# Moving a second layer's conditioning chunks from the first projections into two norms and a later stage, with three expert chunks loaded ahead, in a two-layer fp32 trunk

## What is computed

```
c_act = silu(c)
for l in range(2):
    mod = c_act @ w_ada[l] + b_ada[l]                 # 24 chunks of 1 MB a layer: "conditioning"
    sh1, sc1, gt1, sh2, sc2, gt2 = split(mod, 6)
    h = x * (1 + sc1) + sh1
    y = token_mixer(h, ...)                           # one input projection w_in, gMLP and HGRN2 heads, w_out
    x = layer_norm(ALPHA * x + gt1 * y)
    h = x * (1 + sc2) + sh2
    f = swiglu(h) if l == 0 else moe_swiglu(h)        # dense of width 2816, then top-2 of 8 experts
    x = layer_norm(ALPHA * x + gt2 * f)
```

## Time and profile before

| what | value |
|---|---|
| runs before | 1508.42, 1511.43, 1513.97 us |
| the profiled execution | 1511.0 us, of which the span from the first to the last instruction is 1509.2 us |
| mean granted TensorE clock | 0.984 |
| PE busy | 1458.1 us, 97% of the span |
| DVE busy | 1168.5 us, 77% |
| ACT busy | 908.6 us, 60% |
| POOL busy | 46.3 us, 3% |
| share of the chain that ended last | PE 56%, DVE 3%, issue 1%, ACT 1% |
| HBM | 275 GB/s over the span |

### The profile page before, as it was taken

How to read it: one execution, slowest core, us unless ns; L and a number is a source line. 1 busy time by engine, 2 the same in 40 slices (tenths; PEclk the granted TensorE clock), 3 DMA queues, 4 the chain that set the end, 5 groups by cost and what they waited for, 6 DMA issues and landing times.

```text
span 1509.2 us, 24798 instructions
## 1 busy us (share of the span) xinstructions
PE 1458.1 (97%) x9804; PEld 1271.8 (84%) x9804; DVE 1168.5 (77%) x1244; ACT 908.6 (60%) x867; POOL 46.3 (3%) x84
## 2 busy tenths in 40 slices
PE   5999999999999999999999999999999999999995
PEld 4899988999998998867888888888878888888884
DVE  1556786556668667859889889898898898988988
ACT  1646565323334665656777676776766766777774
POOL 2000110000000100010000000000000000000000
PEclk7999999999999999999999999999999999999998
DMA  9999467455445742547999999999999999999995
GB/s 329 355 310 338 136 205 262 127 167 167 140 139 188 239 133 64 171 141 255 353 350 352 334 362 337 342 356 333 353 342 333 363 336 341 355 344 365 349 369 194
DMA packets 217751, 416.21 MB, mean 276 GB/s; under 512 B 7919, under 2 KB 79769, under 8 KB 217638
## 3 DMA queue, kind: packets, MB, share of 16 engines
q1 hardware_dynamic: 214086, 402.31, 76.6%
q0 software_dynamic: 3552, 12.33, 2.7%
HBM read 407.80 MB, written 6.82 MB: 275 GB/s over the span
## 4 chain that ended last, share of the span: by engine, by line
PE 56%; DVE 3%; issue 1%; ACT 1%; DMA 0%; DVEq 0%; ACTq 0%
PE bank L702 16%; PE bank L704 16%; PE bank L703 16%; PE bank L1233 1%; PE bank L1271 1%; PE bank L705 1%; PE bank L707 1%; PE bank L706 1%; DVE w_lo L1819 1%; PE bank L1326 1%; PE bank L1327 1%; PE bank L849 0%; PE bank L1182 0%; DMA raw_ring<-in_e_gate_dram 0%; PE bank L1066 0%
## 5 line engine op out<-in xcount | busy, mean ns | idle before, releaser
L1819 DVE TENSOR_TENSOR w_lo<-raw_ring,w_hi 128x2048 fp32r<-128x2048 f32 x265 | 606.6, 2291 | 96.2 <-ACT w_hi L1511 95.6
L1511 ACT ACTIVATE w_hi<-raw_ring 128x2048 fp32r<-128x2048 f32 x266 | 510.5, 1919 | 230.0 <-PE bank L704 219.4
L702 PE MATMUL bank<-w_hi,xg_hi 128*128 128x512 f32 (+1 forms) x768 | 293.2, 382 | 1.2 <-DVE w_lo L1819 1.0
L704 PE MATMUL bank<-w_hi,xg_lo 128*128 128x512 f32 (+1 forms) x768 | 288.9, 376 | 0.0
L703 PE MATMUL bank<-w_lo,xg_hi 128*128 128x512 f32 (+1 forms) x768 | 288.8, 376 | 0.0
L705 PE MATMUL bank<-act_hi,w_hi 128*128 128x320 f32 x720 | 227.2, 316 | 6.2 <-DVE act_lo L1874 5.7
L706 PE MATMUL bank<-act_lo,w_hi 128*128 128x320 f32 x720 | 223.2, 310 | 0.0
L707 PE MATMUL bank<-act_hi,w_lo 128*128 128x320 f32 x720 | 223.1, 310 | 0.0
L1810 DVE TENSOR_TENSOR w_lo<-raw_ring,w_hi 128x2048 fp32r<-128x2048 f32 x65 | 148.6, 2288 | 69.0 <-ACT w_hi L1425 68.9
L704 PEld LDWEIGHTS bank<-w_hi,xg_lo 128*128 128x128 f32 x768 | 144.3, 188 | 29.2
L702 PEld LDWEIGHTS bank<-w_hi,xg_hi 128*128 128x128 f32 x768 | 144.4, 188 | 27.1 <-DVE w_lo L1819 1.4
(11 more groups left out here) (369 smaller groups left out, 1856.2 us busy)
## 6 DMA issues: line engine op xcount, KB each, us to landing
raw_ring<-in_e_gate_dram SPq DMA_DIRECT2D x90, 1024.0 KB, 5.2
raw_ring<-in_e_up_dram SPq DMA_DIRECT2D x90, 1024.0 KB, 5.3
raw_ring<-in_e_down_dram SPq DMA_DIRECT2D x88, 1024.0 KB, 5.3
raw_ring<-in_w_ada_dram SPq DMA_DIRECT2D x32, 1024.0 KB, 7.4
raw_ring<-in_w_in_dram SPq DMA_DIRECT2D x24, 1024.0 KB, 7.2
raw_ring<-in_w_ff_gate_dram SPq DMA_DIRECT2D x11, 1024.0 KB, 5.4
raw_ring<-in_w_ff_up_dram SPq DMA_DIRECT2D x11, 1024.0 KB, 5.2
raw_ring<-in_w_ff_down_dram SPq DMA_DIRECT2D x11, 1024.0 KB, 4.9
```

The source lines that it names most:

```text
L702: pe.matmul(out, xh, wh, start=start, stop=False)
L704: return pe.matmul(out, xl, wh, start=False, stop=stop)
L1511: act.activation(w_hi[:, (NSPLIT + i) % SPL, :], raw[:, s, :], ACT.Copy).then_inc(hi_ready.sem, 1)
L1819: dve.tensor_tensor(w_lo[:, r, :], raw[:, s, :], w_hi[:, r, :].bitcast(F32), ALU.subtract).then_inc(lo_ready.sem, 1)
```

## The change

1. **First projections of layer 0.** `GROUPS` no longer holds four of its pairs: one of two at w = 6, and those at w = 8, 9 and 10. Layer 0's own chunks to 23 stay. `modulation(0, 1)` follows at w = 8.
2. **Norms.** `LATE` is (8, 8, 4, 4): chunks 24 to 31 in norm (0, 0), 32 to 39 in norm (0, 1) and `win_first`, 40 behind w = 3 of layer 1 and 41 to 43 behind w = 9, m = 1; 44 to 47 stay in norm (1, 0). All `keep_busy` calls go. Layer 1's chunks are taken in another order (`ada_chunk`), so that what `modulation(1, 1)` needs is complete with 43.
3. **Slots.** The moved chunks are loaded into seven buffers that are dead at that time (`spare`), each with its own wait in SP's list (`spare_free`).
4. **DVE.** `modulation(1, 0)` goes from layer 0's output projection to chunk c = 1 of the dense channel mixer; `modulation(1, 1)` from w = 1 of layer 1's projections to the head of layer 1's output projection.
5. **ACT.** The two copies `ada_rows` behind `modulated` of layer 1 move inside it.
6. **Experts.** Chunks 4, 5 and 6 are loaded before the loop into three buffers (`ahead_sil`, `ahead_y`, `behind_hf`). The first buffer is that of `sil`, so the first silu waits until chunk 4 has been split. At the end of a round SP waits for the last scatter and loads the three again, and the fifth output waits for these loads.
7. Semaphores of the final norm are merged.

```diff
-    for w in range(2, NWIN - 1):
-        if w == 6:
-            tok = WIN_ORDER[w] // 2 in (1, 4)
-            GROUPS.update({(w, 0): 2, (w, NT - 1 if tok else 1): 2})
-        else:
-            GROUPS.update({(w, 1): 2})
-    LATE = (6, 6, RAW)
+    GROUPS.update({(w, 1): 2 for w in range(2, 8)})
+    LATE = (8, 8, 4, RAW)
...
+    LATE_GROUPS = {(3, 1): [LATE_AT[2]], (9, 1): [LATE_AT[2] + j for j in (1, 2, 3)]}
...
+    def ada_chunk(i):
+
+        l, c = divmod(i, NADA)
+        if l == 0:
+            return l, c
+        return l, c + {3: 4, 4: 3}.get(c // 4, c // 4) * 4 - c // 4 * 4
...
+            if s == EXTRA:
+                return [(qs_mm.sem, qs_mm.at(l, H - 1))]
+            if s == EXTRA + 1:
+                return [(osum_ready.sem, osum_ready.at(l, 1))]
+            if s == EXTRA + 2:
+                return [(mix_lo.sem, mix_lo.at(l, NT))]
+            if s == EXTRA + 3:
+                return [(ix_ready.sem, ix_ready.at(l, H - 1)), (oT_mm.sem, oT_mm.at(l, NT - 1)), (cv_out.sem, 32 * (l + 1))]
+            return [(h_lo.sem, h_lo.at(0, 7))]
...
             def experts(rd):
-                for i in range(RAW, NR + RAW):
-                    expert_load(i % NR, rd * NR + (NSPLIT + i - RAW + 1))
+                for i in list(range(RAW + EARLY, NR)) + list(range(RAW)):
+                    sp.wait_ge(lo_ready.sem, rd * NR + (NSPLIT + moe_before[i] + 1))
+                    expert_load(i)
+                sp.wait_ge(sc_mm.sem, sc_mm.at(rd, NE * KD - 1))
+                for i in range(RAW, RAW + EARLY):
+                    expert_load(i)
...
                         if l and kk in (1, 3):
-                            ada(LATE_AT[1] + (4 if kk == 1 else 5), turn=False)
-                        if l and kk in (3, 7):
+                            ada(LATE_AT[1] + (6 if kk == 1 else 7), turn=False)
+                        if l and kk in (1, 5):
                             ada_turn()
...
                     ada_group(l, w, m)
-                    if (l, w, m) == (0, NWIN - 1, 0):
+                    if l and w == 10:
+                        ada_turn()
+                    if (l, w, m) == (0, MOD_AT, 0):
                         ada_turn()
...
             def norm_end(l, i):
 
-                n0 = LATE_AT[2 * l + i]
+                n0 = LATE_AT[3 * l + i]
                 for j in range(2):
                     ada(n0 + j, turn=False)
                 for m in range(4 if i else KD - 2, KD, 2):
                     pair_sums(l, i, m)
-                if i:
-                    statistics(l, i)
-                    ada_turn()
-                    keep_busy(bank[5], 8)
-                    spread_root(l, i)
-                    keep_busy(bank[5], 8)
-                    ada(n0 + 2, turn=False)
-                    keep_busy(bank[5], 16)
-                    ada(n0 + 3, turn=False)
-                    return
                 ada(n0 + 2, turn=False)
                 statistics(l, i)
                 ada_turn()
                 ada(n0 + 3, turn=False)
                 spread_root(l, i)
                 if l == 0:
-                    keep_busy(bank[7], 12)
+                    for j in range(4, 6):
+                        ada(n0 + j, turn=False)
                 pe.wait_ge(stat_act.sem, stat_act.at(l, 5 * i + ROOT_COPIED))
-                if LATE[2 * l + i] > 4:
-                    ada(n0 + 4, turn=False)
                 ada_turn()
-                if LATE[2 * l + i] > 5:
-                    ada(n0 + 5, turn=False)
+                if l == 0 and i == 0:
+                    for j in range(6, 8):
+                        ada(n0 + j, turn=False)
+                    ada_turn()
...
+                    if l == 0 and i and a < 2:
+                        ada_rows(LATE_AT[0] + 5 + 2 * a)
+                    if l and i == 0 and a in (0, 2):
+                        ada_rows(LATE_AT[1] + 5 + a)
...
                 if l:
-                    ada_rows(LATE_AT[1] + 3)
-                    ada_rows(LATE_AT[1] + 5)
                     make_hi(base + 2)
...
+                if n == 0:
+                    act.wait_ge(lo_ready.sem, rd * NR + (NSPLIT + RAW + 1))
                 act.activation(sil2[:, b % 2, 0:w], bank[1 + b % 2][:, 0:w], ACT.Silu).then_inc(e_silu.sem, 1)
...
-                    if w == 1 and l:
-                        modulation(l, 1)
+
...
                 make_lo(base + 1)
+                if l:
+                    modulation(l, 1)
...
-                    if m == 1 and l == 0:
-                        modulation(1, 0)
...
+                        if c == 1:
+                            modulation(1, 0)
                         product(c)
```

More of the change, by code:

```diff
@@ L147, in hybrid_trunk @@
         landed[key] = (s, 16 * times[s])
-    RAW_USES = times[:RAW]
-    MOE_RAW0 = ring
-    assert NR % SPL == 0 and NR % RAW == 0 and all(w % CW == 0 for _, w in EB)
+    EARLY = 3
+    AHEAD0 = NSLOTS
+    times += [0] * EARLY
+    moe_slots, moe_turns, moe_before, uses, last_in = [], [], [], [0] * len(times), [None] * len(times)
+    for i in range(NR):
+        s = AHEAD0 + i - RAW if RAW <= i < RAW + EARLY else (ring + i - (0 if i < RAW else EARLY)) % RAW
+        moe_slots.append(s)
+        moe_turns.append(uses[s])
+        moe_before.append(last_in[s])
+        uses[s] += 1
+        last_in[s] = i
+    for i in range(RAW):
+        moe_before[i] = last_in[moe_slots[i]]
+    assert NR % SPL == 0 and all(w % CW == 0 for _, w in EB)
     with ExitStack() as ctx:
@@ L243, in hybrid_trunk @@
             sil, aa = (a[:].rearrange("p c n -> p (c n)")[:, 0:2 * T] for a in (sil2, aa2))
+            with ExitStack() as cx:
+                ff_spare = sb("ff_spare", [P, 3, SLOT], c=cx)
+            spare += [ff_spare[:, i, :] for i in range(3)]
             lg = sb("lg", [P, 8, NT, NE], c=c2)
@@ L286, in hybrid_trunk @@
         lt_exp = signal("lt_exp")
-        raw_in = [signal(f"raw_in{i}") for i in range(RAW + 2)]
+        raw_in = [signal(f"raw_in{i}") for i in range(AHEAD0 + EARLY)]
         hi_ready = signal("hi_ready")
@@ L412, in hybrid_trunk @@
         f_by_rs = signal("f_by_rs")
-        out_done = [signal(f"out_done{i}") for i in range(2 * NT)]
+        rows_done = signal("rows_done")
+        pool_rows_done = signal("pool_rows_done")
         outs = signal("outs")
@@ L472, in load @@
                     sp.wait_ge(lo_ready.sem, old[1] + 1)
-                what = ("ada",) + divmod(key[1], NADA) if key[0] == "ada" else split_keys[key[1]]
+                if s >= EXTRA:
+                    for free in spare_free(s, 0):
+                        sp.wait_ge(*free)
+                what = ("ada",) + ada_chunk(key[1]) if key[0] == "ada" else split_keys[key[1]]
                 sp.dma_start(slot_as(raw_slot(s), what[0]), chunk_source(*what)).then_inc(raw_in[s].sem, 16)
@@ L515, in _ @@
                 if n < RAW:
-                    sp.wait_ge(raw_in[n].sem, rounds * (16 * NR // RAW) + 16 * (RAW_USES[n] + 1))
-                sp.wait_ge(out_done[n].sem, 1)
+                    sp.wait_ge(*expert_in(rounds, n))
+                elif n == RAW:
+                    for i in range(RAW, RAW + EARLY):
+                        sp.wait_ge(*expert_in(rounds, i))
+                if n in POOL_OUT:
+                    sp.wait_ge(pool_rows_done.sem, POOL_OUT.index(n) + 1)
+                else:
+                    sp.wait_ge(rows_done.sem, n - len(POOL_OUT) + 1)
                 dst = y_prompt[0, t0:t0 + nt, cols] if t < 2 else y_sample.rearrange("b s d -> (b s) d")[:, cols]
@@ L741, in ada_group @@
             def ada_group(l, w, m):
-                for i in group_ada.get((w, m), []) if l == 0 else []:
-                    ada(i)
+                for i in (LATE_GROUPS if l else group_ada).get((w, m), []):
+                    ada(i, turn=(l == 0))
             def split_chunk(key):
@@ L1562, in _ @@
                             ada_rows(i)
+                        if (l, w, m) == (1, 10, 0):
+                            ada_rows(LATE_AT[2] + 3)
                     if w == 1:
```

129 lines of the change are left out of this document (76 added, 53 removed).

## The result

The changed kernel has a median of 1516.35 us over 12 runs (1513.93 to 1518.26), the kernel before 1511.47 us over 12 (1508.42 to 1516.03). The ratio is 1.0028, with a 95% interval of 1.0017 to 1.0039: it is slower, by 4.2 us by the ratio and 4.9 by the medians, and outside the predicted range of 1501.5 to 1513.5. (The ratio is worked out from all executions and isn't that of the two medians; the two can differ by some 2 us.) Its profiled execution took 1514.17 us with a span of 1512.4, 3.2 more than that of before.

What follows compares the result with a forecast made beforehand. PE was taken as the bound, busy 97% and without a gap in the experts. Terms −4.4 − 1.1 − 0.1 + 0.65 + 0.85 + 1.0 = −3.1 gave 1508.4 us on the median's footing, range 1501.5 to 1513.5.

Steps and rivals of the forecast that it cites:

- first projections: Layer 0's first projections: four pairs leaving them change the time by −4.4 us, bounds −8.8 and −2.2.
- norm (0, 0): Norm (0, 0): PE's DMA wait goes and the modulation leaves DVE, together −1.1 us.
- norm (0, 1): Norm (0, 1): `act_lo` ends it, not the dummies; −0.1 us without a clock fall, bounds −0.3 and +1.1.
- head and projections of layer 1: Layer 1's head: new 2.1 us stall for `w_lo` and added chunks, partly given back; +0.65 us, bounds −1.0 and +2.7.
- output projection: Layer 1's output projection: the modulation on DVE delays PE's first sums, +0.85 us, bounds 0 and 1.45.
- first silu: Start of the experts: the first silu waits for chunk 4's split, +1.0 us, bounds 0 and 1.8.
- end of the loop: End of a round: three added 1 MB loads cost 0, or +3 us if they land after the fifth output leaves.
- The first rival: First projections: all of the pairs' time, 8.8 us, comes back, giving 1502.9 us; chance 0.2.
- The −2.25: Layer 0, w = 8 to 11: without three pairs it behaves as layer 1, −2.25 us with the clock's fall.
- −3.9: The same stretch of layer 0 without the clock's fall: −3.9 us (2.25 + 1.7).
- The second rival: Clock falls ahead of layer 1's first product and in the stall before L792: 1511.8 up to 1515.2 us; chance 0.22.
- Early chunks: Start of the experts' loop: chunks loaded ahead bring at most the 0.8 us that PE waits there.

Runs made afterwards that it cites:

- run 1: Changed kernel with the slots put right: expert chunk i from 7 on in ring slot i mod 4; 1509.80 us, ratio 0.9981 to the kernel before.
- run 3: Changed kernel without its part in the experts: no chunk loaded ahead, no added wait at the first silu; 1509.13 us, ratio 0.9972.
- run 4: As run 1, with ACT's second copy at the head of layer 1 behind all four parts of the modulation; 1506.62 us, ratio 0.9957.
- run 5: As run 1, with 14 dummy products on PE in the stall for `w_lo`; 1508.46 us, ratio 0.9981; again 1508.07 us, ratio 0.9977.
- run 9: As run 8, with expert chunks 4 and 5 loaded ahead, slots put right, no wait at the first silu; 1502.02 us, ratio 0.9940.
- run 2: Kernel before, with chunk 0's reload waiting for the split of the round's last expert chunk; 1518.27 us, ratio 1.0031.
- run 8: Changed kernel without its experts part, copy behind four parts, modulation (1, 1) in w = 10, layer 0's last pair at w = 9; 1502.43 us, ratio 0.9940.
- run 1 repeated: The kernel of run 1 measured once more, on one chip with the repeat of run 5; 1508.77 us, ratio 0.9986.

## Why the prediction was wrong

The sum was right to the end of the loop and had one term there at nothing that was 6.3 us.

| term | predicted | by the rows |
|---|---|---|
| first projections | −4.4 | −4.8 (of which 0.2 was there ahead of it) |
| norm (0, 0) | −1.1 | −1.0 |
| norm (0, 1) | −0.1 | +0.4 |
| head and projections of layer 1 | +0.65 | +0.4 |
| output projection | +0.85 | +0.75 |
| first silu | +1.0 | +1.2 |
| sum up to the last round's end | −3.1 | −3.1 |
| end of the loop | 0 | +6.3 |

That −3.1 met −3.1 is in part luck. The terms are off by up to 0.5 us and cancel, and the clock of the profiled execution did what the sum had assumed: low behind the wait for `S` in layer 0, high at the two new idle stretches. In the profiles of runs 1, 3, 4, 5 and 9 it fell in other places, at 1.3 to 1.6 us each.

- **The step that failed** is the end of a round: "At the end of a round three 1 MB loads are added after the last scatter ... 0, or +3 if they don't." I looked at the loads that were added and not at those whose slot was moved. The term was put at 0, and it measured +6.3. Taking three chunks out of a ring of four shifts each later chunk by three, and the first reload of the next round then hangs on the round's last chunk. The price is one DMA's landing (6.09 us of ACT's wait), because ACT's copies of the next round stand ahead of this round's last `y_hi`. Runs 1 and 2 show it.
- **First projections: right.** PE idles 2.44 us for `S` at 145.56, as layer 1's row said, and three pairs bring 2.2 us and not 6.6. The first rival, all of the pairs' time, is ruled out; run 8 shows the other side of it, a pair that costs 0.5 us there. (The rival's own sum had the first silu at 0 where mine had +1.0, without a reason; with it, it is 1503.9.) The −2.25 was that of a low clock, and the clock was low here (0.50 from 146 to 148 us); in the profiles where it wasn't, PE left the place some 1.6 us sooner, near the −3.9 that the prediction gave for that case.
- **Norm (0, 0): right.** The DMA wait is gone, and the first product waits 0.15 us for `act_lo`.
- **Norm (0, 1): off by 0.5.** PE waited 1.63 us for a DMA into `ff_spare` ahead of the last chunk, and that chunk with its turn ran until the first product at 480.69, while `act_lo` was ready at 480.12. So the chunk's load, which I had taken as early enough, ended the norm, some 0.4 us late (an estimate from these rows). I had also misread: the first product at 486.10 shows no wait, it follows the last chunk (485.08 and 1.08 long), and `act_lo` was ready at 485.71. The clock stayed at 1.00 behind it, as I had chosen over the rule of the Trainium skill; but in the profiles of run 4, of run 5 and of run 9 it was 0.50 there, at a cost of 1.3 to 1.5 us. The choice held for this execution and not for the kernel.
- **Head of layer 1: right** (+0.4 for +0.65). ACT stood 4.60 us at the copy, `w_lo` was late, PE waited 1.90 us (predicted 2.1). The three chunks fill the wait for `S` there (570.50 to 573.25), and the level behind them has no wait.
- **The second rival, the clock, is partly true.** In the changed kernel's profile no fall followed the stall; in those of runs 1 and 3 one did. Behind the wait at 145 us it fell in the profiles of the changed kernel, run 1 and run 3, and not in those of run 4, run 5 and run 1 repeated. The Trainium skill, TensorE: Matmul & The Clock Gate, section What's actually happening, has the clock lifted by recent activity and throttled without it; the windows of run 4 agree (0.50 behind the stall, 1.00 without it), but the same 1.90 us idle was followed by 1.00 in the changed kernel's profile and in that of run 1 repeated. It may hold a part of the difference between the profile's +3.2 and the medians' +4.9 us; that was only argued, and the interval of the ratio (+2.6 to +5.9 us) has room for both.
- **Early chunks: they bring nothing.** The prediction gave them at most 0.8 us; run 9 shows by its rows that without their costs they bring none of it.

What was left of the change when its two mistakes (slots, copy) and its misplaced modulation were mended, and one pair moved into the wait, is a kernel 0.6% faster than before: 1502.4 us.

## What to carry to other kernels

When some items are taken out of a ring, follow the slot of every item behind them, and above all which item the first of the next round now waits for: the loads that are added are easy to see, and those that are only renumbered decide. An instruction that prepares the next round and stands ahead of the last one of this round makes its DMA part of this round's end. And work that must go somewhere goes where the engine waits for a chain of others: the same pair cost 2.0 us in dense work and 0.5 in such a wait.

## What the runs showed of the hardware

PE idle for 1.90 us was followed by a granted clock of 0.50 (1.2 GHz) in one execution of run 1's kernel and by 1.00 (2.4 GHz) in another; behind the 2.44 us for `S` in layer 0 it was 0.50 in the profiles of three kernels (changed, run 1, run 3) and 1.00 in six other profiles, run 1's kernel among them. At the end of norm (0, 1), late in or behind an idle stretch of 1.6 us, it was 0.50 in three profiles (runs 4, 5 and 9) and 1.00 in those of the changed kernel and run 1, with the same idle time. Where it fell at 146 us, PE left the place 1.6 us later against the run of dummies, which had no fall there (row against row). Behind the stall the fall cost 1.5 us against the run of dummies, and in norm (0, 1) 1.3 to 1.5. So executions of one kernel can differ by that much for this alone. 14 dummy products in the stall (1.68 of 1.90 us) went with a clock of 1.00 in both profiles that had them; a stall without them had that too, in two of four.
